# Feed-forward norm in a two-block transformer: the root applied where gate and up leave PSUM, tiles rounded behind attention's output, modulation groups on halves of the up stages

## The reference, cut to what matters

```
h = x + jnp.concatenate([gla_out, nsa_out], axis=-1) @ w_out
m = rms_norm(h, ffn_norm_g)          # h * rsqrt(mean(h*h) + EPS) * g
return h + (jax.nn.silu(m @ w_gate) * (m @ w_up)) @ w_down

m = jax.nn.silu(cvec) @ w + b        # modulation of the second block
```

## Time and profile before

| | us |
|---|---|
| median of 3 runs (lowest to highest) | 2297.34 (2293.23 to 2301.37) |
| the profiled execution | 2291.27 |
| its span | 2289.6 |
| TensorE busy | 2117.3 |
| VectorE busy | 1555.8 |
| ScalarE busy | 883.9 |

### The profile page before, as it was taken

The page is one execution under the profiler, slowest core; times in us unless marked ns, Lnnn a source line. Parts: engine busy times, 40 slices in busy tenths (PEclk is TensorE's granted clock), DMA queues, the critical chain, the costliest instruction groups (busy, mean ns, idle before and its releaser), DMA issues.

```text
span 2289.6 us, 43648 instructions
## 1 busy us (share of the span) xinstructions
PE 2117.3 (92%) x16374; PEld 2058.1 (90%) x16374; DVE 1555.8 (68%) x2031; ACT 883.9 (39%) x1154; POOL 169.3 (7%) x268
## 2 busy tenths in 40 slices
PE   5999987389979999999999999899999996979997
PEld 5999986368979999999999999899889996979997
DVE  4788464547879558675566758767777777667855
ACT  4333331244343333333333345315545344333442
POOL 0000000001200000000000002100000120000011
PEclk8999977569979999999999999999999998989998
DMA  4568521005748568785587756446435882536752
GB/s 172 183 234 278 185 83 46 0 1 178 263 151 272 195 223 274 240 274 194 201 271 261 274 193 213 169 163 212 143 134 200 270 272 95 183 115 226 264 183 93
DMA packets 119549, 434.04 MB, mean 190 GB/s; under 512 B 13216, under 2 KB 13600, under 8 KB 119216
## 3 DMA queue, kind: packets, MB, share of 16 engines
q1 hardware_dynamic: 90672, 328.11, 42.0%
q0 software_dynamic: 28800, 104.87, 13.1%
HBM read 430.83 MB, written 2.10 MB: 189 GB/s over the span
## 4 chain that ended last, share of the span: by engine, by line
PE 83%; DVE 12%; issue 2%; ACT 2%; DMA 1%; POOL 0%; DVEq 0%; SPq 0%; POOLq 0%; ACTq 0%
PE ps L474 24%; PE ps L475 24%; PE ps L476 24%; DVE w_lo L1186 2%; PE ps L534 2%; PE ps L529 1%; DVE mod_sum L1202 1%; PE ps L820 1%; PE ps L830 1%; PE ps L571 1%; DVE sq L1255 1%; PE ps L540 1%; PE ps L702 1%; DVE rstd L1247 0%; DVE a_lo L1263 0%
## 5 line engine op out<-in xcount | busy, mean ns | idle before, releaser
L908 ACT ACTIVATE w_hi<-raw 128x1024 fp32r<-128x1024 f32 x610 | 635.0, 1057 | 715.0 <-PE ps L476 704.5
L474 PE MATMUL ps<-a_hi,w_hi 128*128 128x256 f32 x3024 | 864.2, 286 | 46.6 <-DVE w_lo L1186 22.8
L475 PE MATMUL ps<-a_lo,w_hi 128*128 128x256 f32 x3024 | 861.1, 285 | 0.0
L476 PE MATMUL ps<-a_hi,w_lo 128*128 128x256 f32 x3024 | 860.8, 285 | 0.0
L1186 DVE TENSOR_TENSOR w_lo<-raw,w_hi 128x1024 fp32r<-128x1024 f32 x610 | 740.5, 1256 | 130.3 <-ACT w_hi L908 127.7
L474 PEld LDWEIGHTS ps<-a_hi,w_hi 128*128 128x128 f32 x3024 | 583.7, 193 | 50.5 <-issue 24.6
L475 PEld LDWEIGHTS ps<-a_lo,w_hi 128*128 128x128 f32 x3024 | 583.8, 193 | 0.0
L476 PEld LDWEIGHTS ps<-a_hi,w_lo 128*128 128x128 f32 x3024 | 583.6, 193 | 0.0
L474 PE MATMUL ps<-b_hi,w_hi 128*128 128x256 f32 x1920 | 554.2, 289 | 18.9 <-DVE w_lo L1186 7.6
L475 PE MATMUL ps<-b_lo,w_hi 128*128 128x256 f32 x1920 | 547.3, 285 | 0.0
L476 PE MATMUL ps<-b_hi,w_lo 128*128 128x256 f32 x1920 | 547.2, 285 | 0.0
(11 more groups left out here) (269 smaller groups left out, 1336.7 us busy)
## 6 DMA issues: line engine op xcount, KB each, us to landing
raw<-w_main SPq DMA_DIRECT2D x610, 512.0 KB, 4.3
side<-w_side POOLq DMA_DIRECT2D x200, 512.0 KB, 4.5
x_tok<-x_in SPq DMA_DIRECT2D x4, 512.0 KB, 6.1
ctx_tok<-ctx_tok SPq DMA_DIRECT2D x1, 2048.0 KB, 10.2
y_out<-o_tok SPq DMA_DIRECT2D x4, 512.0 KB, 2.7
cons<-cons_in SPq DMA_DIRECT2D x1, 542.0 KB, 8.1
table<-counts_tab SPq DMA_DIRECT2D x1, 512.0 KB, 11.0
table<-masks_in SPq DMA_DIRECT2D x1, 448.0 KB, 12.3
```

The costliest lines, as they stand in the source:

```text
L474: pe.matmul(out_ap, wh, act_hi[:, kt, :], start=first and n == 0, stop=False)
L475: pe.matmul(out_ap, wh, act_lo[:, kt, :], start=False, stop=False)
L476: mm = pe.matmul(out_ap, wl, act_hi[:, kt, :], start=False, stop=last and n == len(blocks) - 1)
L908: act.activation(w_hi[:, slot, :], raw[:, slot, :], ACT.Copy).then_inc(hi_ready, 1)
```

## The change

**The norm.** In the output stage ScalarE now rounds `res` times gain directly into `a_hi` behind each read, before it squares the tile, and VectorE makes `a_lo` of the tile before (`ffn_rest`). The root is not in these tiles. Up stages start without it. The sum of squares is made behind up0's first step (`norm_sums`), mean, root and reciprocal follow in the first read of up0, and every result of an up stage is multiplied by the root as it leaves PSUM, into a new pair of tiles `up_x`. The silu reads `up_x` where it read PSUM, and waits for VectorE's read where it waited for TensorE. The product of silu and up tile reads `up_x` too.

**The stages.** up0 and up1 are each split into two stages of 16 steps (up0b, up1b), so that each half can carry a modulation group. The groups move: out and ev_q carry none, up0b and up1b do. Groups 1, 2 and 3, with two vectors, are now on up0, up0b and down0; before they were on out, up0 and down0. The steps of up stages now count in `dve_read`; before they did not. SP's wait before down0 (`sp.wait_ge(dve_read, dve_reads("down0"))`, ahead of the loads of context, counts and down0's weights) is unchanged in its text and so takes in the up0 stages' reads.

```diff
 assert sum(CHUNKS) == FFN_TILES
+UPS = (("up0", "up0b"), ("up1", "up1b"), ("up2",))
 SCALE = DH ** -0.5
...
 STAGES = [("conv", 16), ("rest", 29), ("out", 16),
-          ("up0", 32), ("down0", 16), ("up1", 32), ("down1", 16), ("up2", 24), ("down2", 16),
+          ("up0", 16), ("up0b", 16), ("down0", 16), ("up1", 16), ("up1b", 16),
+          ("down1", 16), ("up2", 24), ("down2", 16),
           ("ev_kv", 8), ("ev_q", 16), ("ev_z", 16), ("ev_out", 16),
...
-MOD_GROUPS = {"rest": 0, "out": 1, "up0": 2, "down0": 3, "up1": 4, "down1": 5, "up2": 6,
-              "ev_kv": 7, "ev_q": 8, "ev_z": 9, "ev_out": 10, "od_z": 11}
+MOD_GROUPS = {"rest": 0, "up0": 1, "up0b": 2, "down0": 3, "up1": 4, "up1b": 5, "down1": 6, "up2": 7,
+              "ev_kv": 8, "ev_z": 9, "ev_out": 10, "od_z": 11}
 MOD_STAGES = list(MOD_GROUPS)
...
     return DT // min(DT, COUNT[stage])
-MOD_BANK = {"ev_kv": 4, "ev_q": 6}
+MOD_BANK = {"ev_kv": 4}
 BOTH = (0, 1, 2, 3)
...
             return n
-        n += 0 if name[:2] == "up" or name[-2:] == "_z" else count
+        n += 0 if name[-2:] == "_z" else count
...
     return 16 * NORMS.index(name) + tile + 1
+def scaled(name, tile):
+    return normed(name, tile) - (16 if name in ("ev", "od") else 0)
...
+        up_x = at("up_x", PR + 36 * K, [P, 2, T])
         sg = at("sg", PR + 40 * K, [P, 1, T])
...
-            mods_and_squares(CMP_AT + 2, 0)
-            mod_loads(CMP_AT + DT + 2, group_start("ev_kv") + 2)
+            for k in range(16):
+                add_square(0, k)
+            mod_loads(CMP_AT + 2, group_start("ev_kv") + 2)
             for k in range(16):
...
-            def run(stage, act, kt=16, second=None, split=None, summed=None, chain=None):
+            def norm_sums(name):
+                pe.wait_ge(S("squares_added"), 16 * SUMMED.index(name) + 16)
+                pe.matmul(ps[:, 2, 0:T], ones, sq_sum[:, :], start=True, stop=True).then_inc(S("sums_ready"), 1)
+            def run(stage, act, kt=16, second=None, split=None, summed=None, chain=None, before=None):
...
                         next(chain)
+                    if before is not None and isinstance(i, int) and k == 0:
+                        norm_sums(before)
                 steps(pe, stage, body, first=COUNT[stage] if chain is not None else 2 if split else 0)
                 if summed is not None:
-                    pe.wait_ge(S("squares_added"), 16 * SUMMED.index(summed) + 16)
-                    pe.matmul(ps[:, 2, 0:T], ones, sq_sum[:, :], start=True, stop=True).then_inc(S("sums_ready"), 1)
+                    norm_sums(summed)
                 if stage in MOD_GROUPS:
...
             pe.wait_ge(S("mix_lo"), 1)
-            run("out", (b_hi, b_lo), summed="ffn")
+            run("out", (b_hi, b_lo))
...
                 silus = sum(CHUNKS[:c])
-                pe.wait_ge(dve_read, dve_reads(f"up{c}"))
-                def body(i, k, c=c, silus=silus):
-                    step(f"up{c}", i, k, (a_hi, a_lo),
-                         free=(S("gate_y"), i + (silus + 1)) if k % 2 else (silu_ready, i + (silus + 1)),
-                         split=[("norm_lo", normed("ffn", -1))] if c == 0 and isinstance(i, int) and k == 0 else None)
-                steps(pe, f"up{c}", body, first=0 if c else 2)
-                sum_mods(f"up{c}")
+                for name in UPS[c]:
+                    first = name == "up0"
+                    run(name, (a_hi, a_lo), split=[("norm_lo", normed("ffn", -1))] if first else None,
+                        before="ffn" if first else None)
                 last = c == len(CHUNKS) - 1
...
                             pe.wait_ge(S("e_rot"), j + 2)
-                        if t == Z0:
-                            pe.wait_ge(S("mods_read"), MOD_STAGES.index("ev_q") + 1)
                         rotate(rot_g[:, 0, :] if j < 4 else con("rot"), 16 + 2 * j, 6)
...
-        def gate_silu_steps(act, stage, silus):
+        def gate_silu_steps(act, stage, silus, root):
...
                 s = FIRST[stage] + k
-                act.wait_ge(halves_used, i * 4 + (2 * s + 2))
-                act.wait_ge(S("gate_y"), i + (silus + 1))
-                act.activation(sg[:, 0, :], ps[:, s % 2, 0:T], ACT.Silu).then_inc(silu_ready, 1)
+                if s == FIRST["up0"] and isinstance(i, int):
+                    root("ffn", rstd[:, :])
+                    act.activation(warm[:, :], ident[:, 0:2], ACT.Silu).then_inc(silu_ready, 1)
+                act.wait_ge(dve_read, i * 2 + (dve_reads(stage) + k + 1))
+                act.wait_ge(S("gate_y"), i + (silus + k // 2 + 1))
+                act.activation(sg[:, 0, :], up_x[:, 0, :], ACT.Silu).then_inc(silu_ready, 1)
             return extra
...
-            def ahead(stage, first=0, extra=None, squared=None, of=None, chain=None):
+            def ahead(stage, first=0, extra=None, squared=None, of=None, chain=None, rounded=False):
...
                     act.wait_ge(dve_read, i * 2 + (base + k + 1))
+                    src = of[:, k:k + 1, :] if isinstance(i, int) else of[:, bass.ds(i * 2 + k, 1), :]
+                    if rounded:
+                        a = COLS["ffn_g"][0] + k
+                        dst = a_hi[:, k:k + 1, :] if isinstance(i, int) else a_hi[:, bass.ds(i * 2 + k, 1), :]
+                        gain = cols[:, a:a + 1] if isinstance(i, int) else cols[:, bass.ds(i * 2 + a, 1)]
+                        act.activation(dst, src, ACT.Copy, scale=gain).then_inc(S("norm_hi"), 1)
                     if not isinstance(i, int) or k >= 2:
                         act.wait_ge(S("squares_added"), i * 2 + (16 * SUMMED.index(squared) + k - 1))
-                    src = of[:, k:k + 1, :] if isinstance(i, int) else of[:, bass.ds(i * 2 + k, 1), :]
                     act.activation(sq_tile[:, k % 2:k % 2 + 1, :], src, ACT.Square).then_inc(S("squared"), 1)
...
                     first = 4
-                if chain is not None:
+                if chain is not None or rounded:
                     first = COUNT[stage]
...
                 for f in range(16):
-                    act.wait_ge(S("norm_y"), normed(name, f))
+                    act.wait_ge(S("norm_y"), scaled(name, f))
                     if shift is None:
...
-            ahead("out", squared="ffn", of=res)
-            root("ffn", rstd[:, :])
-            shift_hi("ffn", sq, a_hi, None)
-            act.activation(sg[:, 0, 0:2], ident[:, 0:2], ACT.Silu).then_inc(silu_ready, 1)
+            ahead("out", squared="ffn", of=res, rounded=True)
             def ctx_chain():
...
             for c, n in enumerate(CHUNKS):
-                ahead(f"up{c}", extra=gate_silu_steps(act, f"up{c}", sum(CHUNKS[:c])))
+                for part, name in enumerate(UPS[c]):
+                    ahead(name, extra=gate_silu_steps(act, name, sum(CHUNKS[:c]) + 8 * part, root),
+                          first=2 if name == "up0" else 0)
                 if c < len(CHUNKS) - 1:
...
-            def reading(stage, read, first=0, splits=(), between=None, chain=None):
+            def reading(stage, read, first=0, splits=(), between=None, chain=None, after=None):
...
                       last=2 if stage == "od_out" else 0, splits=splits, between=between)
+                if after is not None:
+                    after()
                 if each:
...
-            reading("out", add_res)
-            norm("ffn", res, sq, lambda f: col("ffn_g", f), None, a_hi, a_lo)
+            rstd_row = rstd[:, :].rearrange("p (a t) -> p a t", a=1)
+            def ffn_rest(i, k):
+                dve.wait_ge(S("norm_hi"), i * 2 + normed("ffn", k))
+                a = COLS["ffn_g"][0] + k
+                gain = cols[:, a:a + 1] if isinstance(i, int) else cols[:, bass.ds(i * 2 + a, 1)]
+                dve.scalar_tensor_tensor(out=tile(a_lo, i, k), in0=tile(res, i, k), scalar=gain,
+                                         in1=tile(a_hi, i, k).bitcast(F32), op0=ALU.mult, op1=ALU.subtract)\
+                   .then_inc(S("norm_lo"), 1)
+            def out_read(i, k, bank):
+                add_res(i, k, bank)
+                if k == 0:
+                    return
+                dve.wait_ge(dve_read, i * 2 + (dve_reads("out") + k))
+                ffn_rest(i, k - 1)
+            reading("out", out_read, first=2, after=lambda: ffn_rest(0, 15))
             dve.memset(gated[:, 0, :], 0.0).then_inc(S("gate_y"), 1)
...
-                def up_read(i, k, bank, done=done):
-                    if k % 2:
-                        split_out(i, 1, done + k // 2, psum_tile(bank), k // 2)
-                reading(f"up{c}", up_read)
+                for part, name in enumerate(UPS[c]):
+                    def up_read(i, k, bank, name=name, done=done, tile0=8 * part):
+                        if name == "up0" and k == 0 and isinstance(i, int):
+                            mean_to_rstd("ffn", ps[:, 2, 0:T], rstd[:, :], D)
+                        dve.tensor_tensor(up_x[:, k % 2:k % 2 + 1, :], psum_tile(bank), rstd_row, ALU.mult)\
```

(5 more changed lines are left out.)

## The result

The changed kernel takes **2306.99 us** (median of 6 runs, 2305.78 to 2309.83) against 2299.36 us for the kernel before, run beside it (6 runs): 7.6 us or 0.33% more. The ratio that goes with the interval is 1.0039, 95% interval 1.0026 to 1.0053. The kernel is slower by 0.3 to 0.4%. The profiled execution took 2305.78 us, with a span of 2304.1 us.

A forecast was written before the change was run, and what follows sets the result against it. TensorE bounds the kernel now; VectorE's closed loop would bound up0 and up0b. Removed seam, longer periods and sums net +11.1 us on 2291.27, thus 2302.4; that execution lies 6.1 below the median, so 2308 us; own range 2304 to 2313, overall 2283 to 2324.

The forecast's parts named there:

- The seam: Between the output stage's last matmul and up0's first: 25.6 us of TensorE idle and side work, removed by the change.
- the stretch: From the output stage through up0 and up0b to down0's start: +11.1 us, or +7.1 with sums at 4.8 us each.
- the stages behind: Up1, up1b, up2: period some 10.7 us, under 11.52, so free; up1b's added sum 1.8 us, ev_q's removed sum 1.8.
- The loop: Up0 and up0b: a 1.43 us round trip through ScalarE's silu makes VectorE's period 13.14 us per pair against TensorE's 11.52.
- TensorE's idle time: In up0 and up0b: TensorE idles 0.8 us twice per pair, before most steps.
- The sums: At the ends of up0 and up0b: TensorE waits 4.4 us, then 32 small modulation matmuls take 6.8 us.
- rival (b): Loss partly covered, sums at the full clock and some slack regained at the seams: 0 to +7 us, 2297 to 2304; 16%.
- A rule against a row: Up stages' silu-times-up product, now from SBUF: costed at nothing by the trace; the skill's rule would give 0.9 us lower.
- SP's wait: Before down0: wait for VectorE's up reads ends about 844.9, hidden; uncovered up to 5 us. Rival that it shows: 5%.
- (a): Up0 and up0b: round trip hidden, loop not closed, TensorE stays the bound: 20 us faster, 2277; 14%.
- its mild form: Round trip alone falls away, VectorE's 11.71 still exceeds 11.52, seam waits remain: some 14 us faster, 2283; within the 14%.
- (c): Clock falls in the starved loops of up0 and up0b, a slow start every second pair: +15 us more, 2323; 12%.

The follow-up runs named there:

- late silu: Changed kernel with ScalarE taking the gate tile's silu behind the rounding of the next step's weights: 2282.79 us, ratio 0.9933 to the kernel before.
- gate tile first: Changed kernel with VectorE reading the gate tile ahead of its modulation work in even up steps: 2286.33 us, ratio 0.9941 to the kernel before.
- longer trip: Changed kernel with an extra, unused 128x256 ScalarE copy behind every silu: 2320.12 us, ratio 1.0093 to the kernel before.
- experiment 6: Changed kernel with one-vector groups on both up0 halves: 2290.18 us; second run, with the silu also behind the next weights' rounding: 2276.59 us.
- experiment 5: Changed kernel with up0b's modulation group back on the output stage, up0b carrying none: 2303.85 us, ratio 1.0022 to the kernel before.
- experiment 2: The longer trip: changed kernel with an extra, unused ScalarE copy behind every silu: 2320.12 us; its profile windows were compared with the changed kernel's.
- norm alone: Changed kernel with only its norm half, stages and modulation groups as in the kernel before: 2296.50 us, ratio 0.9985 to the kernel before.
- groups alone: Kernel before with up0 and up1 split and groups moved as in the change, norm untouched: 2300.20 us, ratio 1.0006.
- experiment 7: The kernel before, unchanged, profiled a second time: span 2299.1 us.

## Why the prediction was right, and where it was off

- *The seam:* 25.6 us removed, as read. TensorE's timeline shows no gap at the end of the output stage.
- *Luck in the number:* the forecast was +11.1 us on the kernel before, and the medians differ by 7.6. It came to 2308 from a median of 2297.34 in three runs; over six runs that median is 2299.36, 2 us higher, which hides more than half of the miss. The mechanism and the stretch came out as worked out; the stages behind, which were counted at nothing, gave back some 3 us.
- *The loop:* period 13.14 us forecast, 13.19 measured; idle time per pair 1.43 forecast, 1.51 measured (most of the difference is the first leg, 0.10 us from the end of VectorE's product at 705.49 to the silu at 705.59, forecast as 0.04). TensorE was starved in up0b from its seventh step on and not in all 16: the first ones still found their weights ready. That changes nothing in the sum, since VectorE sets when the last modulation tile is there. The late silu (11.59), the gate tile first (11.59) and the longer trip (+0.31 for +0.31) show that the cause is the trip, closed by the order of two queues. Its price depends on both parts: neither the modulation load without VectorE's product in the trip (11.51) nor the trip with half the load (11.52 in up0 of experiment 6) costs anything.
- *TensorE's idle time:* 0.8 us per step forecast. The record prints 0.58, but TensorE's steps in up0 start 6.60 us apart where a full one takes 5.76, so a step loses 0.84; the printed idle time is shorter because the last matmul's record (0.28 us) lasts longer than the distance to the next start (0.12), and the first ones behind the wait take longer.
- *The sums:* 4.4 us of waiting forecast, 4.12 and 4.11 measured; 6.8 us of matmuls forecast, 6.38 and 6.83 measured. Here the row nearest to an idle start was the right one to take, and rival (b), with the sums at the full clock, did not happen. The stretch took 227.7 us, 227.6 forecast; the small misses in it cancel (a longer period, shorter waits and a shorter first sum).
- *A rule against a row:* the product of silu and up tile from SBUF took 0.42 to 0.43 us (the row at 699.00), as it did from PSUM. The 62 cycles, some 65 ns, by which the Trainium skill (VectorE: DVE Perf Modes, the section on the TRN2 errata) has a PSUM source dearer are not to be seen here. In ScalarE's silu there is a difference, and in the other direction: 418 ns from SBUF, 384 from PSUM, as counted in the trip.
- *SP's wait:* hidden in the changed kernel, as forecast, but only since TensorE waits and sums for 11 us at up0b's end. It shows where up0b carries one vector (2.45 us in experiment 6's first run, 2.52 in its second) or none (2.18 in experiment 5), and stays hidden with the late silu and with the gate tile first, whose two-vector sums stand there still.
- *Rivals:* (a) did not happen, but its mild form was priced at 2283 us and the late silu, which makes it true by hand, took 2282.8, though with a period of 11.59 and not 11.71 and 16 us gained on the stretch, not 14. (c) fell: the granted clock stayed at 1.00 in the loop.
- *Missed, small:* ev_q and ev_z give back 1.5 us beyond the sum; I had counted nothing. With up1b's 1.7 the sum is then +11.2 + 1.7 - 3.2 = +9.7 us. From the output stage's first tile to the modulation read behind od_z, which leaves out the earlier part with its wandering clock, the changed kernel took 1655.8 us and the kernel before 1647.4 and 1649.1 in its two profiles, so 6.7 to 8.3 more, like the 7.6 between the medians. The markers place the difference: down0, up1 and up1b together took 285.6 us, against 286.7 and 287.3 before, although up1b's sum adds 1.7. Up1's first step took 5.84 us in the changed kernel's profile and 7.74 and 8.43 in those of before, as told in experiment 2. Whether the change has a part in that clock, one profile of it cannot tell.
- *The two halves of the change do not add up.* Against the kernel before, the norm alone is 3.5 us faster, the groups alone are 0.9 us slower, which is no difference, and both together are 7.6 us slower. Between the norm alone and the changed kernel the output stage up to the mean costs 10.9 us less (no sum at its end), and the stretch from the mean to down0 25.9 us more (221.4 against 195.5): eight more pairs at VectorE's period are 8 x 1.68 = 13.4 us of it. The rest, 12.5, fits the sums: a wait of 4.1 us and a sum of 6.4 between the halves, where the norm alone has neither, and 2.4 us more for the sum at the end. This split is read off the rows and was not tested by a run. I worked none of this out ahead of the runs.

## What to carry to other kernels

When a value that an engine used to read from TensorE is first passed through a second engine, follow both in-order queues until they meet: if the first engine's next duty feeds the second, and the second one's own work fills the period, the trip is added to every period, however idle the first engine is. The cheapest cure is order, not speed: put the consumer's work that others wait for ahead of the waiting instruction. And put a reduction that ends a stage some steps behind the last loaded one: with 16 free steps in between (norm alone) wait and sum at the end of up0's load took 4.5 us, without them 10.5 (changed kernel) and 11.1 (experiment 5).

## What the runs showed of the hardware

- The same program, executed twice, had the granted clock at 0.83 and at 0.50 in the same stretch of the same work (the windows of experiment 7). Ahead of it the two profiles lay 1.0 us apart (modulation reads at 305.17 and 306.19), behind it 7.8 (527.02 and 534.86): a single profile is no measure of differences of this size ahead of the change.
- The 32 modulation matmuls at a stage's end cost 3.63 to 5.72 us where TensorE had idled for 0.7 us or less (5.15 and 5.72 in groups alone, 3.63 at the changed kernel's down0), but 4.55 to 6.99 us behind 2.3 to 2.5 us of idle time (five places), and 6.38 to 6.99 us behind 4.1 to 4.4 us (five).
- Behind the same 32 matmuls at down0's end, with no idle time ahead of them, the next step took 5.84 us in one profile and 7.2 to 8.4 us in the ten others.
- Waits of 0.58 us before nearly every step of up0 left the granted clock at 1.00 all the same.
